# A two-stack model kernel: neighbourhood attention in head pairs with values stationary, and the norms' roots computed by tokens

## The reference, cut to what matters

```python
q, k, v = jnp.split(h @ w_qkv, 3, axis=-1)            # 16 heads of 64
q, k = rms_norm_2(heads(q), q_g), rms_norm_2(heads(k), k_g)
# the same k, v for the 256 context tokens: k_c, v_c
# grid of 8 rows x 64 columns; a query sees 8 rows x 16 columns around it, and all 256 context tokens
s = concat(q @ k_window.T * 0.125 + rpb, q @ k_c.T * 0.125)
o = softmax(s) @ concat(v_window, v_c)
x = x + g1 * (merge(o) @ w_o)
```

```python
x * lax.rsqrt(jnp.mean(x * x, axis=-1, keepdims=True) + EPS)
```

## Time and profile before

| | us |
|---|---|
| median of 3 runs | 3365.1 |
| lowest and highest run | 3318.04 and 3409.23 |
| span of the profiled execution, first to last instruction | 3450.5 |
| TensorE busy in it | 3185.5 (92%) |
| VectorE busy | 1955.3 (57%) |
| ScalarE busy | 1148.3 (33%) |
| GpSimd busy | 401.1 (12%) |

### The profile page before, as it was taken

How to read it: one execution, slowest core, us unless ns; L and a number is a source line. 1 busy time by engine, 2 the same in 40 slices (tenths; PEclk the granted TensorE clock), 3 DMA queues, 4 the chain that set the end, 5 groups by cost and what they waited for, 6 DMA issues and landing times. The chain is left out here.

```text
span 3450.5 us, 37186 instructions
## 1 busy us (share of the span) xinstructions
PE 3185.5 (92%) x14680; PEld 2592.7 (75%) x14680; DVE 1955.3 (57%) x2665; ACT 1148.3 (33%) x1634; POOL 401.1 (12%) x386
## 2 busy tenths in 40 slices
PE   1999988899988999998998999989999899989999
PEld 0777766678867878885677888889877677778887
DVE  4465546756755587776365655576675333344443
ACT  1232224223332342233243322355442333333322
POOL 1000001587411100000010000000000211000000
PEclk9999998999997999999998999999999555589999
DMA  6343322456556455553233444545442100013332
GB/s 212 122 130 114 104 92 75 130 158 196 186 170 208 131 173 175 179 166 109 68 115 123 141 134 131 161 154 183 123 129 79 34 10 10 3 55 104 92 98 86
DMA packets 123373, 419.46 MB, mean 122 GB/s; under 512 B 21456, under 2 KB 21456, under 8 KB 122432
## 3 DMA queue, kind: packets, MB, share of 16 engines
q1 hardware_dynamic: 102672, 372.45, 34.5%
q0 software_dynamic: 10032, 38.35, 3.4%
q10 hardware_dynamic: 10496, 6.29, 0.6%
HBM read 401.37 MB, written 19.86 MB: 122 GB/s over the span
## 5 line engine op out<-in xcount | busy, mean ns | idle before, releaser
L112 PE MATMUL bk<-HH,wh 128*128 128x512 f32 x2176 | 869.5, 400 | 106.4 <-DVE HL L133 83.7
L121 DVE TENSOR_TENSOR wl<-raw,wh 128x1024 fp32r<-128x1024 f32 x506 | 647.2, 1280 | 527.9 <-ACT wh L118 506.2
L112 PE MATMUL bk<-HL,wh 128*128 128x512 f32 x2176 | 859.2, 395 | 0.0
L112 PE MATMUL bk<-HH,wl 128*128 128x512 f32 x2176 | 858.0, 394 | 0.0
L118 ACT ACTIVATE wh<-raw 128x1024 fp32r<-128x1024 f32 x506 | 530.8, 1050 | 436.5 <-PE bk L112 428.9
L112 PEld LDWEIGHTS bk<-HH,wh 128*128 128x128 f32 x2176 | 416.5, 191 | 206.0 <-DVE HL L133 89.5
L112 PEld LDWEIGHTS bk<-HL,wh 128*128 128x128 f32 x2176 | 416.4, 191 | 89.1 <-issue 3.1
L112 PEld LDWEIGHTS bk<-HH,wl 128*128 128x128 f32 x2176 | 415.8, 191 | 88.0
L124 DVE CUSTOM_DVE_ANT_0 ttr<-ar,cB 128x1024 f32<-128x1024 f32 x256 | 331.5, 1295 | 52.7 <-ACT cB L118 28.6
L112 PE MATMUL bk<-gh,wh 128*128 128x512 f32 x704 | 274.5, 390 | 0.0
L112 PE MATMUL bk<-gh,wl 128*128 128x512 f32 x704 | 274.2, 389 | 0.0
(11 more groups left out here) (273 smaller groups left out, 4397.0 us busy)
## 6 DMA issues: line engine op xcount, KB each, us to landing
raw<-in_wts_dram SPq DMA_DIRECT2D x506, 512.0 KB, 3.6
ar<-in_ada_dram SPq DMA_DIRECT2D x192, 512.0 KB, 4.3
F_d<-CA POOLq DMA_DIRECT2D x8, 512.0 KB, 5.3
E_d<-stg POOLq DMA_DIRECT2D x16, 256.0 KB, 4.8
M_d<-K_d POOLq DMA_DIRECT2D x8, 512.0 KB, 12.8
EB<-E_d POOLq DMA_DIRECT2D x8, 512.0 KB, 5.4
EB<-M_d POOLq DMA_DIRECT2D x8, 512.0 KB, 5.0
EB<-F_d POOLq DMA_DIRECT2D x8, 512.0 KB, 5.1
```

The costliest lines, as they stand in the source:

```text
L112: return Nothing() if self.e is None else self.e.matmul(*a, **k)
L121: return Nothing() if self.e is None else self.e.tensor_tensor(*a, **k)
```

## The change

**Attention.** The tokens are ordered in eight blocks of 8 rows x 8 columns (`natural`, `blocks`) and two of them are a query block, so that four neighbouring ones, 256 keys, cover every window; every item has 256 + 256 keys. 32 steps handle two heads each: head 0 on rows 0 to 63 of the array, head 1 on rows 64 to 127, into different banks. The scale is in the gain `nq` of q, which is also negated; one `tensor_tensor_reduce` per head adds the negated bias and takes the minimum over 512 scores. The two copies, TENSOR_REDUCE and the small negation are gone. `values` has the values stationary (128 x 64) and the transposed probabilities moving (128 columns), head 0 on column half 0, head 1 on half 1. The result is feature-major; the divisors are spread, transposed (`divisors`) and multiplied in once per pair. Query blocks 1 and 2 need values at an offset of 64 tokens: GpSimd issues four DMAs that shift them into `Vs`. The bias has buffers for four heads, and its first fetch waits for the context's norm instead of the end of the value products.

**Norms.** `token_sums`: the squares are stationary (128 x 128) and one column of the constant moves, so a token's mean lands on its own partition, in 4 columns. Root and reciprocal work on 128 x 4 (`nst`). `norm_turn` spreads them back with four transposes into a PSUM bank, from which `norm_scaled` reads. The retention's group norm and the heads' norms follow the same pattern; for the latter ScalarE also copies the projection out of PSUM. The steps of the norms that run beside a product are issued at other tiles (`BESIDE`, `EARLY`).

```diff
@@ norms
+        def token_sums(e, b, src, w, start, stop):
+            for tt in range(src.shape[1] // 128):
+                mm = e.matmul(BK[b][:, tt:tt + 1], src[:, tt * 128:tt * 128 + 128], w, start=(start and tt == 0),
+                              stop=(stop and tt == src.shape[1] // 128 - 1))
+            return mm
+        def spread(e, b, col, n):
+            for tt in range(n):
+                mm = e.transpose(BK[b][:, tt * 128:tt * 128 + 128], col[:, tt:tt + 1].to_broadcast([P, 128]), con("ident"))
+            return mm
...
-            e.matmul(BK[b][:, :n.t], con("one1024"), n.ssq[:, :n.t], start=True, stop=False)
+            token_sums(e, b, n.ssq[:, :n.t], w, True, False)
...
-            e.activation(n.rs[:, :n.t], BK[b][:, :n.t], ACT.Sqrt, bias=con("eps"), scale=1.0).then_inc(*act.up(("root", n.tag)))
+            e.activation(n.st, BK[b][:, :n.nt], ACT.Sqrt, bias=con("eps"), scale=1.0).then_inc(*act.up(("root", n.tag)))
...
-            e.reciprocal(n.rs[:, :n.t], n.rs[:, :n.t]).then_inc(*vec.up(("rs", n.tag)))
+            e.reciprocal(n.st, n.st).then_inc(*vec.up(("rs", n.tag)))
@@ heads' norms, odd_pe
+            def roots(n):
+                for i in range(r.turned, r.summed):
...
+                    for tt in range(t // 128):
+                        tr = e.transpose(BK[b][:, tt * 128:tt * 128 + 128], tm[i % 2][:, tt * 128:tt * 128 + 128], con("ident"))
...
+                    for tt in range(t // 128):
+                        mm = e.matmul(BK[b][:, 2 * tt:2 * tt + 2], pr[i % 2][:, tt * 128:tt * 128 + 128], con("blk64")[:, 0:128:64], start=True, stop=True)
@@ attention, odd_pe
+            def scores(s_):
+                p, qb = s_ // 4, s_ % 4
...
+                for part in range(2):
+                    for hf in range(2):
+                        rows = slice(64 * hf, 64 * hf + 64)
+                        b = 2 * hf + s_ % 2
+                        keys = o.Kc[rows, p, :] if part else o.K[rows, p, k0:k0 + 256]
+                        mm = e.matmul(BK[b][:, 256 * part:256 * part + 256], o.Q[rows, p, 128 * qb:128 * qb + 128], keys, start=True, stop=True)
...
+            def turns(s_):
+                for hf in range(2):
+                    claim(e, 4 + hf)
+                    e.wait_ge(*act.of(("ex", s_, hf)))
+                    for q in range(4):
+                        tr = e.transpose(BK[4 + hf][:, q * 128:q * 128 + 128], o.Pr[hf][s_ % 2][:, q * 128:q * 128 + 128], con("ident"))
...
+            def values(s_):
...
+                for q in range(4):
+                    for hf in range(2):
...
+                        mm = e.matmul(BK[b][64 * hf:64 * hf + 64, 128 * qb:128 * qb + 128], va, o.PT[hf][:, q * 128:q * 128 + 128],
+                                      start=(q == 0), stop=(q == 3))
...
+            scores(0)
+            for j in range(NS + 1):
+                if j:
+                    turns(j - 1)
+                if j + 1 < NS:
+                    scores(j + 1)
+                if j and j % 4 == 0:
+                    divisors(j // 4 - 1)
+                if j:
+                    values(j - 1)
@@ attention, odd_vec
+            def largest(i, hf):
...
+                e.tensor_tensor_reduce(two(o.Pr[hf][i % 2][:, :]), two(BK[2 * hf + i % 2][:, :]), o.BM[:, n::12 - n, :], 1.0, 3e38, ALU.add, ALU.min,
+                                       o.nm[:, i % 2, hf:hf + 1]).then_inc(*vec.up(("mx", i, hf)))
@@ attention, odd_act
+                        e.activation(w[:, :], w[:, :], ACT.Exp, bias=o.nm[:, i % 2, hf:hf + 1], scale=-1.0,
+                                     accum_out=o.sm[:, p % 2, n:n + 1]).then_inc(*act.up(("ex", i, hf)))
@@ odd_pool
+            e.wait_ge(*vec.of(("h", "co", 7)))
             e.dma_start(mk[:, :], d["mask"]).then_inc(*d_mk.up("mask"))
+            e.memset(o.BM[:, 12, :], 0.0).then_inc(*pool.up())
...
+                if h == 4:
+                    shifted(e, 0)
+                    shifted(e, 1)
```

More of the change, by code:

```diff
@@ L686, in ret_pe @@
                     var(3)
+            turned(3)
             run(out(3))
@@ L1767, in turn @@
-            def turn(m):
-                claim(e, 7)
-                e.wait_ge(*vec.of(("ov", 8 * m + 7)))
-                for qb in range(4):
-                    mm = e.transpose(BK[7][:, qb * 128:qb * 128 + 128], o.O[m % 2][:, qb, :], con("ident"))
-                mm.then_inc(*pe.up(("tO", m)))
-                bank[7] = (vec, ("ot", m))
-            for i in range(NI + 3):
-                if i < NI:
-                    scores(i)
-                if i >= 3:
-                    values(i - 3)
-                    if i >= 4 and (i - 4) % 8 == 7:
-                        turn((i - 4) // 8)
-                if 0 <= i - 2 < NI:
-                    turns(i - 2)
@@ L1804, in heads @@
                     e.activation(pr[i % 2][:, :t], BK[m % 4][:, :t], ACT.Square).then_inc(*act.up(("qs", key, m)))
-                    if m:
-                        root(key, m - 1, t)
+                    e.activation(DST[key][:, m, :], BK[m % 4][:, :t], ACT.Copy).then_inc(*act.up(("qe", key, m)))
+                    if i and i != 16:
+                        root(i - 1)
                     if beside is not None:
-                        norm_step_act(e, beside, 5, m)
-                root(key, 7, t)
-                if beside is not None:
-                    norm_step_act(e, beside, 5, 8)
+                        for s_ in EARLY.get(m, ()):
+                            norm_step_act(e, beside, 6, s_)
             fence(e, "cf2")
-            heads("q", L, n_o, n_co)
-            heads("kc", LC, n_co)
+            heads("q", n_co)
+            heads("kc")
             for hb in range(2):
@@ L1818, in odd_act @@
                     hi(e, base[("vc", hb)] + q + 2)
+                    if hb == 0 and q == 1:
+                        root(15)
                 for tt in range(2):
@@ L1825, in odd_act @@
                     hi(e, base[("vt", hb)] + q + 2)
+                    if hb == 0 and q == 1:
+                        root(23)
                 for tt in range(4):
@@ L1863, in odd_act @@
             end(act, "odd")
-        QK_AT = [(key, m) for key in ("q", "kc", "k") for m in range(8)]
         def odd_vec(e):
-            def finish(key, m, t, dst, gain):
-                i = NUM[key] + m
-                s_ = pr[i % 2][:, :t]
-                e.wait_ge(*act.of(("qr", key, m)))
-                e.reciprocal(s_, s_).then_inc(*vec.up())
-                e.wait_ge(*vec.now())
-                e.scalar_tensor_tensor(out=dst[:, m, :], in0=BK[m % 4][:, :t], scalar=vec_of(gain), in1=s_, op0=ALU.mult, op1=ALU.mult).then_inc(*vec.up(("qk", key, m)))
-            def heads(key, t, dst, gain, beside=None):
+            while mm_.n < len(MODS):
+                mod_step(e)
@@ L1888, in odd_vec @@
-            heads("kc", LC, o.Kc, "kg")
+                        for s_ in EARLY.get(m, ()):
+                            norm_step_vec(e, beside, s_)
+            e.tensor_scalar(o.nq[:, :], vec_of("qg"), -0.125, None, ALU.mult).then_inc(*vec.up("nq"))
+            e.wait_ge(*vec.now())
+            heads("q", n_co)
+            heads("kc")
             for hb in range(2):
```

529 lines of the change are left out of this document (299 added, 230 removed).

## The result

| | before | after |
|---|---|---|
| median of four runs, us | 3387.16 | 3201.47 |
| lowest and highest, us | 3318.04 and 3439.0 | 3199.48 and 3205.3 |
| span of the profiled execution, us | 3450.5 | 3197.7 |

The ratio after/before is 0.966, with a 95% interval of 0.963 to 0.968. The kernel is faster, by 3.4% against the quicker runs of before and by 5.5% by the medians. Forecast were 3150 us and, against the median of 3365.1 that was known, 6.4%: the gain is smaller than forecast.

What follows compares the result with a forecast made beforehand. TensorE was taken to bound the kernel nearly everywhere, at half clock in the attention. -238 - 20 - 3 - 6 - 5 - 1 = -273 took the 3450.5 us span to about 3177; 3150 was predicted, range 3085 to 3275.

Steps and rivals of the forecast that it cites:

- The attention, -238: Attention: 32 steps of 3.4 us at 2.4 GHz, plus 3 idle and 5 for the clock, 117 us against 355.
- Halves overlap: Attention's scores and values: instructions on two halves of the array run in pairs, scores 1.14 and values 0.99 us per step.
- serial rival: Attention: halves do not overlap, 4.9 us per step, 3225 us by the span; chance 0.08, including the case at 1.2 GHz.
- 2.4 GHz: Attention: the new step, with both halves filled and no load-bound values, gets the full clock, steps of 3.4 us.
- rival with the clock at 1.2 GHz: Attention stays at half clock, 6.4 us per step, 3270 us by the span or 3190 scaled; chance 0.17.
- The fused minimum: Attention, VectorE: 0.69 us plus 0.08 readout per head, leaving TensorE the bound; a slow one was a rival, chance 0.03.
- Norms, -20: Seven norms between products: the first scaled tile comes 2.8 us earlier in each, 20 us in all.
- The retention's heads, -6 and -3: Retention's group norms: last head gains 3 us; the other three heads and the norm beside the context's feed-forward 1.5 each.
- the pauses' clock, -5: Behind the shortened pauses: less time at 1.2 GHz, a guess of 5 us gained (0 to 15).
- Heads' norms, -1: Heads' norms with projections: 10 of 14 idle us regained, 9 more us of TensorE work, net -1 (-8 to +9).
- From the span to the median: Whole kernel: converting the 3177 us span to timed runs, 3150 taken between 3177 and a scaled 3098.
- already taken out: Timed runs below the span: if they had the old attention partly at 2.4 GHz, the median after is 3177 us.

Runs made afterwards that it cites:

- a_one_half: Kernel after, head 0's instructions issued before head 1's, both heads on rows 0 to 63 and column half 0, so nothing can overlap: 3251.2 us.
- a_one_half_late: a_one_half with GpSimd's value shifts ahead of the first mask and bias, for a pause of 12 us at the attention's start: 3263.2 us.
- a_late_bias: Kernel after with the four shifting DMAs ahead of the mask and first bias, so the attention begins with a pause of 12 us: 3212.5 us.
- b_early_bias: Kernel before with the mark that frees the first mask and bias set ahead of the last value products, removing the 9.45 us pause: 3415.5 us.
- a_wide_norms: Kernel after with the seven norms between two products in their old full-tile form, without the turn: 3218.8 us.
- the old form: Kernel after with the retention's group norm as before (root and reciprocal on the full tile, no turn): 3200.9 us.
- the covered turn: Kernel after with ScalarE and VectorE splitting the next unit ahead of the wait for the retention's turn, except for the last head: 3196.5 us.
- b_again: Kernel before, unchanged, run again: 3314 to 3434 us, the profiled execution 3363.4 us.
- a_heads_in_turn: Kernel after with head 0's instructions issued ahead of head 1's in scores and values, instead of interleaved: 3216.0 us.

## Why the prediction was right or wrong

- **What bounds the kernel: right.** The attention was the stage at half the clock, and it gave 240 us of the 252.8.
- **The attention, -238: right against the profile**, measured -240 (355.0 to 114.7), in part by luck. The forecast's 3.4 us per step is 3.31 and 0.11 for the divisors. TensorE's own work is 3.11 (scores 1.06 for 1.14; values 1.03 with the change of shape, for 0.99 and 0.1; transposes 1.02 with theirs, for 0.88 and 0.1) and 0.15 for the divisors, 3.26. The waits for VectorE in every fourth step bring the mean back to 3.41. The start cost 2.48 us of idle time and 3.4 us at 1.2 GHz, for the 3 and 10 that the record takes.
- **Halves overlap: right**, and priced: 47 us of the attention, 50 by the runs (a_one_half). The serial rival is excluded.
- **2.4 GHz: right, for a reason that is half wrong.** The record named filled halves and the load-bound part that is gone. On one half the clock rose just as soon (a_one_half_late). What showed an effect is the load-bound values, 17 against 68 us. The rival with the clock at 1.2 GHz fell: a third of the step is transposes, and it rose from 0.50 within 17 us and stayed up (a_late_bias). The Trainium skill (page "TensorE: Matmul & The Clock Gate", section "Part 4: PE-mode transpose") says that the full rate does not engage for transposes. Carried over to this mix of transposes and products, that doesn't hold here; for transposes alone no run here shows it. That the old attention needed the wait at its start to lose the clock isn't so either (b_early_bias).
- **The fused minimum: right.** 684 ns, with 82 for the readout, as taken (0.69 and 0.08). That TensorE stays the bound is right in three steps of four. In the fourth the spreading of the reciprocals, counted at about 0.7 us, takes 0.43 alone and 2.31 beside GpSimd's work on the bias, and TensorE waits: 5 us in all, a term that the record doesn't have.
- **Norms, -20: right in size, by two errors against each other.** a_wide_norms makes it 17.4. The pauses shrank by 4.2 us each, more than the 2.8 counted, 29 in all, and 12 went elsewhere. "0.9 to 1.7 us for the eight sums" was 1.05 in the last norm at 2.4 GHz, but the norm that sums all eight squares by tokens has 64 of them, 13.81 us for 9.71, and had been counted like the others.
- **The retention's heads, -6 and -3, and the pauses' clock, -5: wrong.** This is the second step that failed. It costed the removal of 3.35 us of VectorE and not the wait for the turn, which is queued behind a quarter of a product: 5.69 us in its place. In three heads this cost 9 to 10 us against both the old form and the covered turn, where a gain was forecast; the whole stage lost 7.5 us. With 240.4 from the attention and 17.4 from the norms, all else comes to 5 us lost, where 15 were to be gained (-6, -3, -5, -1).
- **Heads' norms, -1: right.** The stage went from 201.8 to 202.5 us between the same units (the windows view); TensorE's busy time rose from 187.9 to 194.7 us and its idle time fell from 14 to 8, as the two sides of the sum say.
- **From the span to the median: wrong.** This is the step that failed, and the largest error. The attention's 355 us of before are those of a profile that had 1.2 GHz throughout, and the gain of 238 was carried over to timed runs that did not. The sum ended at 3177, and 3150 was put between that and a scaled 3098. In b_again 73 of the 89 us lie in the attention: the reading "already taken out" was the right one, and nothing was to be subtracted. Of the 51 us between 3150 and 3201, 27 are this step, 21 the span (3197.7 for 3177: 23 short outside the attention, 2 more inside it), 2 what a run has around its span (3199.5 for 3197.7), and 2 by which the profiled run lies below the median.
- **3.4% and not 6.4%: the same step.** The ratio counts the quicker runs of before, which lie at 3315 us by it (3201.5 / 0.9657), 50 below the median of 3365.1 that the forecast was set against. So 114 us are gained where 215 were forecast, and of the 101 missing 77 are the spread of before misread (50 and 27). In those runs the old attention had at most some 130 us at 1.2 GHz, as estimated above from their mean clocks, in place of 349, and the change could take about 100 us from it (114 less the 12 of all the rest) in place of 240. That is an estimate; no profile fell in one of them.

## What to carry to other kernels

When a stage runs at half the clock and the timed runs spread, look whether the spread is that stage's: then its gain against the timed runs is smaller than against the profile, and nothing more comes off elsewhere; the mean granted clock of each run tells how much of them ran at the lower level. When a long operation of one engine is replaced by a short one and a turn on another, price the queue in front of the turn; it can be longer than what was removed. Operations that load 128 columns and move few can cost twice: their own time (64 sums in 13.81 us), and the time until the clock returns (one edit here). A VectorE operation with room on average can still stop TensorE where it meets GpSimd's work: look at its single durations, not their mean.

## What the runs showed of the hardware

- Halves overlap across four instructions of issue order: in a_heads_in_turn head 1's scores ran beside head 0's although they stand behind all four of them in the program, at no cost (1.07 us for the scores, 1.06 interleaved). The sixteen values instructions, eight of each head ahead of the other's, cost 1.51 us, against 1.03 interleaved and 1.89 on one half.
- One program's attention had 1.2 GHz for 188 us in one execution and 351 in another, with TensorE busy in 96% or more of both.
- A single edit of operand roles (128 x 64 or 128 x 128 stationary, at about 0.11 us per instruction at 2.4 GHz in both) changed the time to the rise from 17 to 68 us.
- A copy from 8 broadcast columns to 512 took 0.43 us on VectorE alone and 2.31 us where GpSimd's TENSOR_TENSOR overlapped it for 2.1 us, in each of five such copies (2.27 to 2.32), and 0.57 for an overlap of 0.28 (a_one_half). VectorE's copies out of PSUM and fused minima kept 0.69 and 0.68 us beside the same work.
